# Attention: in the first step of each unit, TensorE takes the value products of the step before ahead of the turns

## The chip, the core and the metric

The kernel runs on one core of a Trainium2 chip. Time is device time in microseconds (us) from start to end of one execution. Five engines run their own instruction streams and meet only at semaphores: PE (TensorE, matrix products), DVE (VectorE), ACT (ScalarE), POOL (GpSimd) and SP (SyncE, here a DMA queue). "PEld" in the profile is PE's weight load, which overlaps its products.

## What is computed

One inference step of a hybrid decoder layer. The part that matters here is the attention over the prompt (1024 tokens, 8 query heads of 64, 2 KV heads), with three branches (compressed, selected, sliding window) whose softmax results are weighted by gates and added:

```
s = einsum('btkgd,bskd->bkgts', qg, win_kv[:, :, 0]) - slopes * d_w
p = masked_softmax(s, mask_w)
o_win = einsum('bkgts,bskd->btkgd', p, win_kv[:, :, 1])
...
o = g[:, :, 0] * o_cmp + g[:, :, 1] * o_slc + g[:, :, 2] * o_win
```

The other two branches have the same form over other keys. Around the attention lie the input projection, the convolution group, the compression of the cache, the output projection, an MLP and an embedding gate. Eight sampled sequences (32 rows) have their own attention, which is woven into the steps of the prompt's.

## The kernel before

The attention is the function `attend`. Its work on the prompt is cut into 32 **units** `(g, i)`: for each head pair `g` of 4, for each block `i` of 8 (128 query rows). Block `i` sees more keys the later it is, so a unit has 3, 5, 7, 9, 11, 12, 13 or 14 key blocks of 128. Two key blocks make a **group** `k`, two groups make a **step**; a unit has 1, 2, 2, 3, 3, 3, 4 or 4 steps (i = 0 to 7), 88 steps in all. Units are numbered 0 to 31, so unit 9 is `(1, 1)`; unit 8, 16 and 24 have one step only.

What each engine does for a group, in the order of the data:

- PE `qk(n+2, ch)` (L1815): scores of the unit after next, into one of two pairs of score banks; `score_banks` waits until DVE has read what stood there.
- DVE `scores` (L2076): adds the distance penalty, finds the row minimum, writes `S`.
- ACT `exps` (L1963): exponentials and their sums. ACT issues those of a step's scores one step later (the list `late`).
- DVE `weigh(n+1)` (L2086): reciprocals `inv` of the sums, in step 1 of unit `n` (step 0 if it has one step).
- POOL (L1782): scales `S` by `inv` and the gate, six instructions for a unit.
- PE `turn(k)` (L1827): transposes the scaled weights of a group, into one of three turn banks taken in rotation. It waits for POOL's scaling and for the bank of three turns ago to be kept.
- ACT (L1972, even `k`) or DVE (L2090, odd `k`) `keep(k)`: copies the turned bank to `PT`.
- PE `pv(k)` (L1839): value products, one instruction for each key block and KV head. The profile shows each as 2 records, so a full step of 4 key blocks is x16, and a single key block x4. It waits for `PT` to be kept; the first group of a unit also waits for `o_kept`, as all units sum into the same bank.
- ACT `keep_o(n)` (L1986): copies the finished bank to `mixA`. ACT issues it in the first step of unit `n+1`, behind that step's `keep`, the exponentials of the sampled rows and the late `exps`.

The sampled rows add to some steps: `turn_keys` (L1866, "tk"), kept by ACT (L1975) and DVE (L2093); `quad_scores` (L1874, "qs"), which takes a pair of score banks; `turn_weights` (L1883, "tw"), kept by ACT (L1978); `quad_values` (L1902, "qv"), which waits for that copy.

The order is written out by hand. Every engine takes its instructions in this order of steps; on PE a step `st` of unit `n` reads, cut:

```python
for k in steps[st]:
    turn(k)
...                       # turn_keys(z, 1), turn_weights(z)
for ch in share:
    qk(n + 2, ch)
for k in (steps[st - 1] if st else ()):
    pv(k)
...                       # turn_keys(z, 0), quad_scores, quad_values
```

So the value products of a step run one step late, behind the turns and the scores of the next one, and this holds across the border of two units too.

Of the kernel before, what the change touches and what calls it, by code (L numbers as in the profile page):

```python
# [1566 lines left out]
def attend(c, ps):  # L1567
# [60 lines left out]
    steps = [[m for m in range(a, min(a + 2, first_group[n + 1]))] for n in range(NU) for a in range(first_group[n], first_group[n + 1], 2)]  # L1628
# [4 lines left out]
    def with_step(n):  # L1633

        ns = first_step[n + 1] - first_step[n]
        nch = len(CHUNKS[n + 2]) if n + 2 < NU else 0
        return [[ch for ch in range(nch) if ch * ns // nch == j] for j in range(ns)]
# [7 lines left out]
    def quad_at(st, after_start):  # L1645

        return next((z for z in range(NZ) if START[z] + after_start == st), None)

    def weighed_at(st):

        return next((z for z in range(NZ) if START[z] + (4 if place(z) == 0 else 3) == st), None)

    def chosen_at(st, after_start):
        return next((gr for gr in range(2) if CHOOSE[gr] + after_start == st), None)
# [133 lines left out]
    def on_pe(pe):  # L1788
# [8 lines left out]
        def is_kept(t):  # L1797
            pe.wait_ge(kept[keeper(t)], keeps[turn_no[t]])
# [7 lines left out]
        def qk(n, ch):  # L1806
            g, i = UNITS[n]
            s = score_banks(("p", n, ch))
            off = 0
            for br, k0, w in CHUNKS[n][ch]:  # L1810
                for e in range(KVH):
                    rows = slice(DH * e, DH * e + DH)
                    w0 = P * max(0, i - 4)
                    keys = c.KcP[rows, :] if br == 0 else c.proj[rows, KS, k0:k0 + w] if br == 1 else c.proj[rows, KW, w0 + k0:w0 + k0 + w]
                    mm = nc.tensor.matmul(ps_S[:, s + e, off:off + w], c.q[rows, g, P * i:P * i + P], keys, start=True, stop=True)  # L1815
                off += w
            mm.then_inc(qk_done, 1)

        def turn(k):
            n, b0 = groups[k]  # L1820
            blocks = BLOCKS[n][b0:b0 + 2]
            if n:
                pe.wait_ge(scaled, 6 * n - 6 + max({1: 2, 2: 4, 0: 6}[br] for br, _, _ in blocks))
            ps = bank(("p", k))
            for j, (_, _, col) in enumerate(blocks):
                for e in range(KVH):
                    mm = nc.tensor.transpose(ps[:, P * (2 * j + e):P * (2 * j + e) + P], S[UNITS[n][1]][:, e, col:col + P], c.ident[:])  # L1827
            mm.then_inc(t_done, 1)

        def pv(k):  # L1830
            n, b0 = groups[k]
            is_kept(("p", k))
            if b0 == 0 and n:
                pe.wait_ge(o_kept, n)
            for j, (br, kb, _) in enumerate(BLOCKS[n][b0:b0 + 2]):
                for e in range(KVH):
                    rows = slice(DH * e, DH * e + DH)
                    v = c.VcP[:, rows] if br == 0 else c.V[:, kb, br - 1, rows]
                    mm = nc.tensor.matmul(ps_O[rows, 0:P], v, PTs[k % 4][:, P * (2 * j + e):P * (2 * j + e) + P],  # L1839
                                          start=(b0 + j == 0), stop=(b0 + j == len(BLOCKS[n]) - 1))  # L1840
            if k + 1 == first_group[n + 1]:
                mm.then_inc(pv_done, 1)

        def first_scores(gr):

            s = score_banks(("f", gr))
            for bb in range(GRP):
                b = GRP * gr + bb
                rows = slice(ROWS * bb, ROWS * bb + ROWS)
                nc.tensor.matmul(ps_S[rows, s, 0:256], c.QB[:, b, :], c.KcS[:, b, :], start=True, stop=True)  # L1850
                nc.tensor.matmul(ps_S[rows, s, 256:256 + SR], c.QB[:, b, :], c.KnT[:, 0, :], start=True, stop=True)
                mm = nc.tensor.matmul(ps_S[rows, s, 256 + SR:256 + 2 * SR], c.QB[:, b, :], c.KnT[:, 1, :], start=True, stop=True)
            mm.then_inc(qk_done, 1)

        def importance(gr):
            pe.wait_ge(imp_ready, gr + 1)
            ps = bank(("i", gr))
            nc.tensor.matmul(ps[:, 0:64], Gm[:], imp[:], start=True, stop=True).then_inc(t_done, 1)

        def turn_keys(z, half):  # L1860
            h = 2 * z + half
            pe.wait_ge(raw_loaded[h % 5], arrived(h))
            for bb in (2 * half, 2 * half + 1):
                ps = bank(("k", z, bb))
                for j in range(4):
                    mm = nc.tensor.transpose(ps[:, P * j:P * j + P], page(h, bb, j)[:, 0:P], c.ident[:])  # L1866
                mm.then_inc(t_done, 1)

        def quad_scores(z):
            s = score_banks(("s", z))  # L1870
            for bb in range(GRP):
                is_kept(("k", z, bb))
            for bb in range(GRP):
                mm = nc.tensor.matmul(ps_S[ROWS * bb:ROWS * bb + ROWS, s, :], c.QB[:, GRP * group_of(z) + bb, :], KT_[bb][:], start=True, stop=True)  # L1874
            mm.then_inc(qk_done, 1)

        def turn_weights(z):
            pe.wait_ge(sx_done, sx_after(z))
            if place(z) == 0:
                pe.wait_ge(win_scaled, group_of(z) + 1)  # L1880
            ps = bank(("q", z))
            for j in range(4):
                mm = nc.tensor.transpose(ps[:, P * j:P * j + P], Ss[z % 2][:, P * j:P * j + P], c.ident[:])  # L1883
            mm.then_inc(t_done, 1)
            if place(z) < 2:
                ps = bank(("n", z))
                for j, src in enumerate((Snew[:, 1, :], Pc[:, 0:P], Pc[:, P:2 * P]) if place(z) == 0 else (Snew[:, 0, :],)):
                    mm = nc.tensor.transpose(ps[:, P * j:P * j + P], src, c.ident[:])
                mm.then_inc(t_done, 1)

        def quad_values(z):
            gr = group_of(z)
            ps = bank(("o", z))
            is_kept(("q", z))
            more = []
            if place(z) < 2:
                is_kept(("n", z))
                more = [lambda b: c.Vn[:, 1, :], lambda b: c.VcS[:, 0, b, :], lambda b: c.VcS[:, 1, b, :]] if place(z) == 0 else [lambda b: c.Vn[:, 0, :]]
            for j in range(4):
                for bb in range(GRP):  # L1900
                    rows = slice(ROWS * bb, ROWS * bb + ROWS)
                    mm = nc.tensor.matmul(ps[rows, 0:P], PTq[:, j, rows], page(2 * z + bb // 2, bb, j)[:, P:2 * P],  # L1902
                                          start=(j == 0), stop=(j == 3 and not more))
            for j, v in enumerate(more):
                for bb in range(GRP):
                    rows = slice(ROWS * bb, ROWS * bb + ROWS)
                    mm = nc.tensor.matmul(ps[rows, 0:P], PTn[:, j, rows], v(GRP * gr + bb), start=False, stop=(j == len(more) - 1))
            mm.then_inc(t_done, 1)
# [6 lines left out]
        for n in range(NU):  # L1915
            for j, share in enumerate(with_step(n)):
                st = first_step[n] + j
                for k in steps[st]:
                    turn(k)
                z = quad_at(st, 1)  # L1920
                if z is not None:
                    turn_keys(z, 1)
                z = weighed_at(st)
                if z is not None:
                    turn_weights(z)
                for ch in share:
                    qk(n + 2, ch)
                for k in (steps[st - 1] if st else ()):
                    pv(k)
                z = quad_at(st, 0)  # L1930
                if z is not None:
                    turn_keys(z, 0)
                z = quad_at(st, 1)
                if z is not None:
                    quad_scores(z)
                gr = chosen_at(st, 0)
                if gr is not None:
                    first_scores(gr)
                z = weighed_at(st)
                if z is not None:  # L1940
                    quad_values(z)
                gr = chosen_at(st, 3)
                if gr is not None:
                    importance(gr)
                gr = joined_at(st, 5)
                if gr is not None:
                    turn_out(gr)
# [1762 lines left out]
```

## Time and profile before

| | us |
|---|---|
| median of 3 runs | 1820.42 |
| lowest and highest | 1818.45, 1823.94 |
| the profiled execution, its time | 1820.11 |
| its span, first to last instruction | 1818.5 |
| its granted TensorE clock, mean | 0.991 |
| PE busy in the span | 1760.1 (97%) |
| DVE, ACT, POOL busy | 1206.4, 767.0, 794.3 |
| the attention (`attend`), from and to | 549 to 890 |

The views used are the windows (busy time by engine in a stretch), the waits (who waited for whom, longest first in total) and the timeline (instructions in order of time; in brackets the idle time of the engine before the instruction, and what ended it). An idle time in the timeline is that of the engine; the end of a product is modelled, so the time PE loses is read best from start to start.

### The profile page before, as it was taken

The page shows a single profiled execution, that of the slowest core. Times are in us where ns is not written, and L with a number is a line of the kernel's source. Part 1 is how long each engine was busy: PE and PEld are TensorE (multiplying, and loading weights), DVE is VectorE, ACT ScalarE, POOL GpSimd, SP SyncE. Part 2 cuts the span into 40 slices and gives each one's busy share as a digit, 9 for nine tenths or more (in the row PEclk, how much of TensorE's full clock was granted, in tenths as well). Part 3 has the DMA queues.
Part 4 walks back from the last instruction along what each step waited for, and adds up shares of the span by engine and source line. Part 5 has one row for each costly group of instructions (what it writes and reads, how often), then busy time and mean ns, then how long its engine had stood idle before and what let it go on. Part 6 is the DMA issues. An engine that isn't in the chain of part 4 may idle for free.

```text
span 1818.5 us, 36980 instructions
## 1 busy us (share of the span) xinstructions
PE 1760.1 (97%) x14084; PEld 1639.8 (90%) x14084; DVE 1206.4 (66%) x1909; ACT 767.0 (42%) x1433; POOL 794.3 (44%) x763
## 2 busy tenths in 40 slices
PE   8999999999998999999999899999999999999998
PEld 7999998999995767676899899999999999999998
DVE  6799975675467676767746754555577878845535
ACT  5312332345345665666524333333433333314425
POOL 2204972224303433444544656556555444425531
PEclk9999999999999999999999999999999999999999
DMA  4321365536413444443314223222394632332214
GB/s 157 131 70 47 114 193 145 126 102 164 108 49 117 139 130 123 123 122 112 131 36 148 83 95 120 105 107 95 136 300 144 187 131 87 137 97 74 59 35 142
DMA packets 189983, 214.60 MB, mean 118 GB/s; under 512 B 23012, under 2 KB 152736, under 8 KB 189287
## 3 DMA queue, kind: packets, MB, share of 16 engines
q1 hardware_dynamic: 179357, 188.89, 33.3%
q0 software_dynamic: 7840, 21.25, 4.2%
q8 instruction: 112, 1.84, 0.4%
q10 hardware_dynamic: 2610, 2.10, 0.4%
q14 instruction: 64, 0.52, 0.1%
HBM read 181.22 MB, written 35.55 MB: 119 GB/s over the span
## 4 chain that ended last, share of the span: by engine, by line
PE 54%; DVE 7%; issue 3%; POOL 2%; ACT 2%; DMA 1%; SPq 0%; ACTq 0%; DVEq 0%; POOLq 0%
PE ps L2660 11%; PE ps L3039 8%; PE ps L2665 5%; PE ps L2420 4%; PE ps L3044 4%; PE ps L1827 3%; PE ps L3541 3%; PE ps L200 3%; PE ps L1839 3%; PE ps L1815 3%; POOL S L1782 2%; PE ps L1866 2%; PE ps L3551 1%; PE ps L206 1%; DVE S L2076 1%
## 5 line engine op out<-in xcount | busy, mean ns | idle before, releaser
L1782 POOL TENSOR_SCALAR S<-S,inv,gate_p 128x640 f32<-128x640 f32 (+7 forms) x186 | 124.9, 688 | 192.9 <-DVE inv L2086 192.9
L1166 DVE SCALAR_TENSOR_TENSOR y<-u,conv_w,y 128x1024 f32<-128x1024 f32 x120 | 156.5, 1351 | 1.2
L3039 PE MATMUL ps<-dn_op_hi,dn_hi 128*128 128x264 f32 x672 | 137.9, 287 | 6.8 <-DVE xT L3105 4.7
L433 POOL DMA_DIRECT2D raw<-in_cache_cmp_kv_dram x124 | 77.8, 630 | 151.1 <-DVE relaid L1252 122.4
L1010 PE MATMUL ps_p<-Xhi,w1hi 128*128 128x256 f32 x544 | 139.6, 294 | 1.4 <-ACT Xhi L715 1.4
L3039 PE MATMUL ps<-dn_op_lo,dn_hi 128*128 128x264 f32 x672 | 136.4, 284 | 0.0
L1010 PE MATMUL ps_p<-Xlo,w1hi 128*128 128x256 f32 x544 | 133.2, 284 | 0.0
L1236 DVE TENSOR_TENSOR Xlo<-ps_p,Xhi 128x512 fp32r<-128x512 f32 x132 | 85.1, 685 | 59.6 <-ACT Xhi L715 59.4
L715 ACT ACTIVATE Xhi<-ps_p 128x512 fp32r<-128x512 f32 x132 | 72.4, 598 | 105.5 <-PE ps_p L935 98.1
L3039 PEld LDWEIGHTS ps<-dn_op_hi,dn_hi 128*128 128x128 f32 x672 | 104.2, 189 | 9.2 <-DVE xT L3105 6.0
L1963 ACT ACTIVATE S<-S,mn 128x64 f32<-128x64 f32 (+8 forms) x180 | 108.7, 608 | 2.1 <-DVE mn L2076 2.1
L2660 PE MATMUL ps<-s_hi,up_hi 128*128 128x264 f32 x512 | 104.5, 286 | 3.0 <-ACT rstd L2630 3.0
L1010 PEld LDWEIGHTS ps_p<-Xhi,w1hi 128*128 128x128 f32 x544 | 103.8, 191 | 2.1 <-ACT Xhi L715 1.7
L864 PE MATMUL ps_p<-Ahi,win_hi 128*128 128x352 f32 x456 | 103.8, 327 | 1.5 <-DVE Alo L1143 1.5
L3039 PEld LDWEIGHTS ps<-dn_op_lo,dn_hi 128*128 128x128 f32 x672 | 104.5, 189 | 0.0
L2660 PE MATMUL ps<-s_lo,up_hi 128*128 128x264 f32 x512 | 104.2, 285 | 0.0
L1010 PEld LDWEIGHTS ps_p<-Xlo,w1hi 128*128 128x128 f32 x544 | 103.7, 191 | 0.0
L864 PE MATMUL ps_p<-Alo,win_hi 128*128 128x352 f32 x456 | 103.4, 326 | 0.0
L2974 POOL TENSOR_TENSOR dn_lo<-dn_t_sum,dn_hi 128x512 fp32r<-128x512 f32 x48 | 73.8, 1537 | 66.7 <-ACT dn_hi L2996 66.7
L1827 PEld LDWEIGHTS ps<-ident,S 128*128 128x128 f32 x592 | 64.0, 141 | 37.1 <-issue 19.9
L3044 PE MATMUL ps<-dn_op_hi,dn_lo 128*128 128x264 f32 x672 | 95.9, 285 | 0.0
L1827 PE MATMUL ps<-ident,S 128*128 128x128 f32 x592 | 85.4, 281 | 10.7 <-POOL S L1782 8.0
(502 smaller groups left out, 4911.7 us busy)
## 6 DMA issues: line engine op xcount, KB each, us to landing
s_raw<-in_cache_slc_kv_dram SPq DMA_DIRECT2D x256, 128.0 KB, 2.1
dn_op_raw<-hidden SPq DMA_DIRECT2D x21, 1056.0 KB, 6.3
raw<-in_cache_cmp_kv_dram SPq DMA_DIRECT2D x132, 128.0 KB, 4.2
hidden<-cs SPq DMA_DIRECT2D x32, 528.0 KB, 2.6
up_raw<-in_w_up_dram SPq DMA_DIRECT2D x16, 1024.0 KB, 5.5
raw<-in_cache_cmp_kv_dram POOLq DMA_DIRECT2D x124, 128.0 KB, 4.4
dn_w<-in_w_down_dram SPq DMA_DIRECT2D x48, 256.0 KB, 5.3
win_raw<-in_w_in_dram SPq DMA_DIRECT2D x38, 256.0 KB, 3.3
```

The costliest lines, as they stand in the source:

```text
L433: eng.dma_start(raw[s][DH * half:DH * half + DH, i, :], page.rearrange("o q f -> (o q) f")).then_inc(raw_loaded[0 if g < 2 else part][s], 16)
L864: mm = nc.tensor.matmul(ps[t % 2][:, j, 0:CH], w[t % 2][:, k, :], x[:, k, CH * j:CH * j + CH], start=(m == 0), stop=(m == NG - 1))
L1010: mm = nc.tensor.matmul(ps_h[n % 2][:, 0:w], ws[cc][:, j, :], x[n % 2][:, j % 8, slice(j // 8, j // 8 + w)], start=(j == 0 and m == 0), st ...
L1166: i = V_.scalar_tensor_tensor(out=y, in0=x, scalar=w, in1=y, op0=ALU.mult, op1=ALU.add)
L1236: V_.tensor_tensor(Xlo[n % 2][x], ps_x[v % 2].rearrange("p (n j) -> p j n", j=8), Xhi[n % 2][x].bitcast(F32), ALU.subtract).then_inc(lo_re ...
L1782: nc.gpsimd.tensor_scalar(x, x, inv[:, n % 3, 3 * e + br:3 * e + br + 1], c.gate_p[:, i, H * br + h:H * br + h + 1], ALU.mult, ALU.mult).t ...
L1827: mm = nc.tensor.transpose(ps[:, P * (2 * j + e):P * (2 * j + e) + P], S[UNITS[n][1]][:, e, col:col + P], c.ident[:])
L1963: nc.scalar.activation(x, x, ACT.Exp, bias=mn[:, n % 3, e, br, part:part + 1], scale=-1.0, accum_out=sums[:, n % 3, 3 * e + br:3 * e + br ...
L2660: nc.tensor.matmul(ps[:, bank + j, 0:HC], w_hi[s % 4][:, k, :], ops[m][:, k, c0 + HC * j:c0 + HC * j + HC], start=(k == 0 and m == 0), sto ...
L2665: mm = nc.tensor.matmul(ps[:, bank + j, 0:HC], w_lo[s % 4][:, k, :], ops[0][:, k, c0 + HC * j:c0 + HC * j + HC], start=False, stop=(k == K ...
L3039: nc.tensor.matmul(ps[:, 2 * m + j, 0:HC], w_hi[q % 4][:, k, :], x[:, k, HC * j:HC * j + HC], start=(k == 0 and x is op_hi[n]), stop=False)
L3044: mm = nc.tensor.matmul(ps[:, 2 * m + j, 0:HC], w_lo[q % 4][:, k, :], op_hi[n][:, k, HC * j:HC * j + HC], start=False, stop=(k == KH - 1))
```

## The change

In the first step of each unit but the very first, the loop that issues `pv` for the step before stands ahead of the turns. In all other steps it stays behind the scores. Nothing is added or removed: the same instructions with the same waits, in another order on PE. ACT, DVE, POOL and SP keep theirs.

```diff
             for j, share in enumerate(with_step(n)):
                 st = first_step[n] + j
+                opens = j == 0 and st > 0
+                if opens:
+                    for k in steps[st - 1]:
+                        pv(k)
                 for k in steps[st]:
                     turn(k)
...
                 for ch in share:
                     qk(n + 2, ch)
-                for k in (steps[st - 1] if st else ()):
+                for k in (steps[st - 1] if st and not opens else ()):
                     pv(k)
```

## Rows read from the trace of the kernel before

**Rows 1.** Windows: length, busy us of PE, PEld, DVE, ACT, POOL; clock; DMA.

```profile
549.00:890.00 341.00, 321.81 (x3472) 227.45 (x3473) 243.42 (x806) 221.63 (x601) 147.82 (x217) 0.99 0.40 121
584.00:637.00 53.00, 52.09 (x627) 38.67 (x622) 35.78 (x113) 33.64 (x94) 21.91 (x31) 1.00 0.40 121
```

**Rows 2.** Waits from 545 to 890: who for whom, us in total, times, longest.

```profile
PE ps L1827 <- POOL S L1782: 8.0, 11, 1.3
PE ps L1839 <- ACT mixA L1986: 3.5, 5, 1.5
ACT mixA L1986 <- PE ps L1839: 14.0, 16, 2.2
```

**Rows 3.** Timeline of PE and ACT, first and second step of unit 9: start, us, instruction.

```profile
643.34 1.09 PE L1827 MATMUL ps<-ident,S 128*128 128x128 f32 x8
644.03 0.60 ACT L1972 ACTIVATE PT<-ps 128x512 f32<-128x512 f32 x1 [1.75 <-PE ps L1827]
644.37 1.99 PE L1815 MATMUL ps<-proj,q_back 64*128 64x512 f32 x8
...
646.28 0.66 PE L1839 MATMUL ps<-PT,V 128*64 128x128 f32 x8
...
647.09 0.44 PE L1827 MATMUL ps<-ident,S 128*128 128x128 f32 x2
...
648.67 0.25 ACT L1986 ACTIVATE mixA<-ps 128x128 f32<-128x128 f32 x1
...
649.07 1.09 PE L1839 MATMUL ps<-PT,V 128*64 128x128 f32 x16 [0.73 <-ACT mixA L1986]
```

**Rows 4.** Timeline of PE and ACT, first and second step of unit 6.

```profile
613.12 1.09 PE L1827 MATMUL ps<-ident,S 128*128 128x128 f32 x8
613.82 0.60 ACT L1972 ACTIVATE PT<-ps 128x512 f32<-128x512 f32 x1 [3.04 <-PE ps L1827]
617.68 0.26 ACT L1986 ACTIVATE mixA<-ps 128x128 f32<-128x128 f32 x1
618.08 1.09 PE L1839 MATMUL ps<-PT,V 128*64 128x128 f32 x16 [0.56 <-ACT mixA L1986]
```

**Rows 5.** Timeline, first step of unit 4: its turns, and the copy before them.

```profile
584.49 1.09 PE L1827 MATMUL ps<-ident,S 128*128 128x128 f32 x8
585.25 0.41 DVE L2090 COPY PT<-ps 128x256 f32<-128x256 f32 x1
```

**Rows 6.** Timeline, first step of unit 12: scores, their reading, value products, quad scores.

```profile
674.43 1.77 PE L1815 MATMUL ps<-proj,q_back 64*128 64x512 f32 x8
675.61 0.75 DVE L2076 CUSTOM_DVE_ANT_0 S<-ps,far_selected,neg_slope 128x512 f32<-128x512 f32 x1 [0.38 <-PE ps L1815]
676.30 0.44 PE L1839 MATMUL ps<-PT,VcP 128*64 128x128 f32 x4
677.09 1.07 PE L1874 MATMUL ps<-s_KT,QB 128*32 128x512 f32 x8 [0.35 <-DVE mn L2076]
```

**Rows 7.** Timeline, unit 21: DVE's scores, its key copy, the key turns after it.

```profile
777.26 0.75 DVE L2076 CUSTOM_DVE_ANT_0 S<-ps,far_selected,neg_slope 128x512 f32<-128x512 f32 x1 [0.31 <-PE ps L1815]
780.08 0.69 DVE L2093 COPY s_KT<-ps 128x512 f32<-128x512 f32 x1
780.91 1.07 PE L1866 MATMUL ps<-ident,s_raw 128*128 128x128 f32 x8
```

**Rows 8.** Timeline, end of unit 18 and the turns that open unit 19.

```profile
748.13 1.09 PE L1839 MATMUL ps<-PT,V 128*64 128x128 f32 x16
750.51 1.09 PE L1827 MATMUL ps<-ident,S 128*128 128x128 f32 x8 [1.30 <-POOL S L1782]
```

**Rows 9.** Timeline, first step of unit 30: weights turned, kept, used.

```profile
872.59 0.60 PE L1883 MATMUL ps<-ident,s_S 128*128 128x128 f32 x4
873.22 0.60 ACT L1978 ACTIVATE s_PTq<-ps 128x512 f32<-128x512 f32 x1 [0.28 <-PE ps L1883]
874.14 1.08 PE L1902 MATMUL ps<-s_raw,s_PTq 128*32 128x128 f32 x32
```

## Prediction

> **What bounds the kernel now.** I read the windows first, then PE's waits, then the timeline around each of the 31 unit borders. The windows show the attention as a stretch of 341.00 us in which PE is busy for 321.81 us, while DVE, ACT and POOL have 243.42, 221.63 and 147.82 us of work [rows 1]. So the attention is set by PE's in-order stream and the 19.2 us in which it stands still. The waits name two of these that the change touches: turns that wait for POOL's scaling, 8.0 us in 11 places, and the first value products of a unit that wait for ACT's copy of the unit before, 3.5 us in 5 places [rows 2]. Outside the attention no instruction changes place.
>
> **What is moved, and its length.** Turns of a full step hold PE from 643.34 to 644.37, 1.03 us; two full score chunks 1.91 us; value products of three key blocks 0.81 us (646.28 to 647.09) [rows 3]. A full step of products shows 1.09 us, whose last 0.06 to 0.07 overlaps what follows, so 1.02 us. By key blocks the move carries at each border: 0.54 (i=0), 0.81 (i=1), 0.37 (i=2), 0.81 (i=3), 0.37 (i=4), 0.81 (i=5), 1.02 (i=6), 0.37 (i=7). The short ones are estimates by key block. Summed over 31 borders this is 19.7 us of PE work ahead of turns and scores. PE's total work is the same; what changes is that turns and scores come later by the moved length, and that nothing stands any more between the scores and what follows them. Each has a price where another engine had no slack.
>
> **Gain: waits that are filled.** At unit 19 the last products start at 748.13 and are issued by 749.15; the turns start at 750.51, held by POOL [rows 8]. The 0.81 us of products fit in these 1.36 us. Going border by border, such a wait exists at units 2, 3, 10, 17, 19, 25, 26 and 27, and min(wait, moved length) sums to 4.6 us. That is the whole intended gain, since POOL's wait is only 8.0 us in all [rows 2], and part of it lies at turns that open no unit.
>
> **Cost 1: the result copy comes later.** In unit 9's first step ACT idles 1.75 us for the turn, then works without a gap until the copy of unit 8's result at 648.67, and PE's first products of unit 9 start right behind it at 649.07, after 0.73 us of waiting [rows 3]. That copy shows no wait for the products it copies: ACT is what is late, through `keep` and the late exponentials, all behind the turn. With 0.81 us of products ahead of the turn, ACT's chain and those products come 0.81 later. In unit 6 it is the same with 1.02 us: idle 3.04 before 613.82, copy at 617.68, products at 618.08 [rows 4]. Only 16 of 31 copies wait for PE [rows 2]; at these the move helps ACT by as much, and nothing is lost. Of the other 15 most have slack. Priced with each one's slack: unit 1 0.81, unit 6 1.02, unit 9 0.81, unit 11 0.13, unit 14 1.01, unit 22 0.62 (it returns as a wait for a turn bank two steps on).
> The Trainium skill's page "PSUM — Partial Sum Buffer" says under "Engine vs sequencer instructions" that ScalarE's queue is strictly first in, first out. By that rule the copy can't pass the exponentials, and the price stands; if it could, this term of about 4.4 us would be nothing and the sum about 3.3 us over the time before. The rows agree with the rule.
>
> **Cost 2: the preceding step isn't kept yet.** At 584.49 PE is ready to open unit 4. The last group of unit 3 is kept by DVE from 585.25 to 585.66 [rows 5]. Before, that was needed only behind two score chunks; now PE waits 1.3 us with everything behind it. Some 0.3 of this comes back at the next turns, so 1.0 us. At all other borders the copies end 0.3 us or more before PE arrives.
>
> **Cost 3: score banks.** In unit 12's first step the quad scores at 677.09 already wait for DVE to read the first chunk, which DVE begins 1.18 us behind the start of the scores at 674.43 [rows 6]. The 0.37 us of products at 676.30 covered part of this wait. Moved ahead, they push the scores and the reading 0.37 later and cover nothing: plus 0.37, likewise at units 18 and 20; at unit 8 0.54. At unit 26 the filled 0.37 is lost to the same wait.
>
> **Cost 4: turn banks behind DVE.** In unit 21 DVE goes from the scores at 777.26 without a gap to the key copy at 780.08; the next key turns start at 780.91, as that bank is free [rows 7]. Scores 0.81 later give 0.78, likewise in unit 29. In unit 10 the stretch is of this kind too (0.1 net).
>
> **Cost 5: the tail.** In unit 30 there are no scores. The turned weights (872.59) are copied by ACT from 873.22 to 873.82, and PE uses them at 874.14, behind the value products that now lie ahead [rows 9]. The copy comes 1.02 later and ends at 874.84, so PE waits until 874.96: 0.82. POOL's last scaling, which sets the end of the attention, moves with it. Unit 31 has slack and costs nothing.
>
> **Sum, cycle by cycle** (a filled wait counts only if nothing behind it gives it back):
> - units 1 to 7: 0.81 lost at unit 1, given back by filled waits at 2 and 3; plus 1.00 (unit 4) plus 1.02 (unit 6): 2.0
> - units 8 to 15: 0.54 + 0.81 + 0.10 + 0.13 + 0.37 + 1.01: 3.0
> - units 16 to 23: the fill at 17 is swallowed by DVE's load in the next step, 0.37 at 18, minus 0.81 at 19, then 0.37 + 0.78 + 0.62: 1.3
> - units 24 to 31: about 0.6 by unit 26 (later copies and scores), minus 0.81 at 27, then 0.78 + 0.82: 1.4
>
> Together 7.7 us slower. Against the profiled execution's 1820.11, which is 0.31 below the median, this gives 1827.8; against the median 1828.1. I take 1828.0, 0.42% up. Behind the attention comes the output projection, where PE is busy without a gap, so nothing there takes it back.
>
> **The rivals.**
> *A, the border is filled and nothing is behind it.* If ACT and DVE have more slack than their gapless stretches suggest, the 4.6 us stand, and the earlier end of a unit's products also frees the result copy, which would remove the 3.5 us of [rows 2]: 1820.4 - 8.1 = 1812.3. It decides where ACT's copies waited for PE; 16 did, but the five that hold PE did not [rows 3, 4]. Chance 0.06.
> *B, absorbed.* Half or more of the shifts vanish in waits that end on their own, or fills hold where I let them be swallowed: between 1815 and 1825.8, at the middle 1821. Of PE's 19.2 us of idle time 11 are outside the two waits named, which speaks for it; that ACT and DVE are themselves started by PE there speaks against it. Chance 0.32.
> *C, every shift is paid in full.* 19.7 us less 4.6 gives 1835. Against it stand the 16 copies that wait for PE. Chance 0.06.
> *D, the clock.* Around the borders turns now follow turns more closely. The granted clock is 1.00 in a stretch that holds seven borders [rows 1]. The Trainium skill's page "TensorE: Matmul & The Clock Gate" says under "Part 4: PE-mode transpose" that transposes don't count as activity for the clock. By it long runs of turns would drop PE to 1.2 GHz. Without the page: a border of about 5 us at half the clock costs up to 5 us, and at a few of them the time would be about 1845. Such runs of turns and key turns stand in that stretch already at full clock. Chance 0.01.
>
> **Chances and range.** Forecast (1825.9 to 1832) 0.55, A 0.06, B 0.32, C 0.06, D 0.01. A measurement of this kernel can tell some 0.3% (5.5 us) from no change: slower 0.62, same 0.32, faster 0.06. The range reaches into B and C: 1818.5 to 1834.
>
> **What would show it.** Right: the first products of units 6, 9 and 14 start 0.8 to 1.0 later behind their turns, PE's wait for the result copy (3.5 us) grows to 7 or more, its wait for POOL (8.0) shrinks to about 4; the products that open unit 4 wait 1.3 us for DVE; quad scores in units 8, 12, 18 and 20 wait longer for DVE. Wrong: copies that start no later than before, or an attention no longer than 341 us. The prediction falls above all if ACT's exponentials start on something other than the turn.

## The result, and the profile after

The changed kernel takes 1827.65 us (median of 6, 1824.1 to 1829.74) against 1820.02 (6 runs of the kernel before, beside them): ratio 1.0032, 95% interval 1.0019 to 1.0046, slower by 3.5 to 8.4 us. The two medians lie 7.6 us apart; the middle of the interval is 5.8 us. Predicted were 1828.0. Its profiled execution has 1826.1 us and a span of 1824.4.

The windows of the attention after the change (columns as in [rows 1]: length, busy time of PE, PEld, DVE, ACT, POOL with counts, clock, DMA):

```profile
549.00:896.50 347.50, 319.68 (x3460) 227.40 (x3462) 242.63 (x806) 218.24 (x600) 147.19 (x217) 1.00 0.40 117
```

The window grew from 341.0 to 347.5 us. Both are cut at round times; from the attention's first turn to the first product of the output projection it is 340.59 before and 347.54 after. PE's work did not grow (321.81 in [rows 1], part of it at a lower clock, 319.68 here); its idle time did, from 19.2 to 27.8. PE's waits from 545 to 900 (who for whom, us in total, times, longest; those that changed most) say where:

```profile
PE ps L1839 <- ACT mixA L1990: 7.8, 8, 1.9
PE ps L1874 <- DVE mn L2080: 3.8, 5, 1.0
PE ps L1827 <- POOL S L1782: 3.2, 6, 0.6
PE ps L1866 <- DVE s_KT L2097: 3.2, 3, 1.5
PE ps L1902 <- ACT s_PTq L1982: 2.1, 3, 0.8
PE ps L1839 <- DVE PT L2094: 1.2, 1, 1.2
PE ps L1827 <- DVE PT L2094: 1.0, 1, 1.0
PE ps L1827 <- DVE mixA L2172: 0.6, 1, 0.6
```

Lines behind the diff are 4 higher than before: L1990 is the copy of the result that was L1986. Against [rows 2], the turns' wait for POOL fell from 8.0 to 3.2 us. Not all of these 4.8 us are gain. At the openings of units 3, 17, 19, 26 and 27 it shrank by 3.5, which the moved products filled. At unit 2 another 1.05 went because PE came there late and at a lower clock (last section), at unit 31 0.87 because PE now waits for DVE there, and at unit 22 0.61 is new. The wait for the result copy rose from 3.5 to 7.8, and quad scores (L1874) waiting for DVE rose from 1.8 (before) to 3.8, in 5 places both times. Key turns waiting for DVE (L1866 behind `s_KT`) rose from 1.1 to 3.2, and a wait of 1.2 for DVE's `PT` in front of value products is new, as are the last two lines, the turns of unit 31 behind DVE. What was filled is paid back more than twice over. The first products of unit 4, the quad scores of unit 12 and the key turns of unit 21 show one each of these waits:

```profile
585.54 0.44 PE L1839 MATMUL ps<-PT,VcP 128*64 128x128 f32 x4 [1.23 <-DVE PT L2094]
680.79 1.06 PE L1874 MATMUL ps<-s_KT,QB 128*32 128x512 f32 x8 [0.72 <-DVE mn L2080]
786.89 1.07 PE L1866 MATMUL ps<-ident,s_raw 128*128 128x128 f32 x8 [0.84 <-DVE s_KT L2097]
```

Unit 6 shows one price in full. PE and ACT, first and second step (start, us, instruction; in brackets the idle time before it and what ended it):

```profile
614.67 1.09 PE L1827 MATMUL ps<-ident,S 128*128 128x128 f32 x8
615.37 0.60 ACT L1976 ACTIVATE PT<-ps 128x512 f32<-128x512 f32 x1 [4.06 <-PE ps L1827]
619.22 0.26 ACT L1990 ACTIVATE mixA<-ps 128x128 f32<-128x128 f32 x1
619.62 1.09 PE L1839 MATMUL ps<-PT,V 128*64 128x128 f32 x16 [1.58 <-ACT mixA L1990]
```

Against [rows 4]: ACT starts 0.70 us behind the turn in both, and the copy starts 3.85 (before 3.86) behind that. Only PE changed places: it has nothing left to do behind the scores and waits 1.58 instead of 0.56. The difference, 1.02, is the length of the moved products. So the unit's first products do not start later behind its turns (4.95 us, before 4.96): turns, copy and products are all 1.02 late together.

**The lag table.** The timeline gives the start of the turns of each of the 88 steps. The lag of a step is its start in a kernel less its start in before, less the same difference at the attention's first turn. What a border costs is the change of the lag across its unit, counted from the end of unit 0 on. Two profiled executions of one order agree in this to about 0.02 us per unit, with a drift of 0.15 over the whole attention, apart from a few places where the granted clock falls (e0_none, below). By groups of units:

| units | forecast | measured |
|---|---|---|
| 1 to 7 | +2.0 | +2.40 |
| 8 to 15 | +3.0 | +3.16 |
| 16 to 23 | +1.3 | +1.28 |
| 24 to 31 | +1.4 | +1.46 |
| sum | +7.7 | +8.30 |

The first product of the output projection comes at 897.19 instead of 889.59. These 7.60 us are the 8.30, plus 0.65 by which the attention's first turn was late (549.65 instead of 549.00), less 1.35 that before's profile loses in unit 0, where its granted clock is 0.54.

### The profile page after: what moved, and what is told of

Same layout as the page of the kernel before. It is cut to its first block, busy times and chain, and to the rows that moved or that the text cites. A ratio compares the mean times of both kernels' runs of the same rounds, so it can differ in the third digit from the quotient of the medians.

```text
span 1824.4 us, 36980 instructions
## 1 busy us (share of the span) xinstructions
PE 1759.5 (96%) x14084; PEld 1640.6 (90%) x14084; DVE 1206.7 (66%) x1909; ACT 764.8 (42%) x1433; POOL 794.4 (44%) x763
## 4 chain that ended last, share of the span: by engine, by line
PE 54%; DVE 8%; issue 4%; POOL 2%; ACT 2%; ACTq 0%; DVEq 0%; POOLq 0%
PE ps L2664 11%; PE ps L3043 8%; PE ps L2669 6%; PE ps L2424 4%; PE ps L3048 4%; PE ps L3545 3%; PE ps L200 3%; PE ps L1839 3%; PE ps L1827 3%; PE ps L1815 2%; POOL S L1782 2%; PE ps L3555 1%; PE ps L206 1%; DVE S L2080 1%; PE ps L1866 1%
```

## The experiments

The theories: the **ledger** of the prediction (each border has its own price, by what another engine lacks there), the **spread** theory (the loss is a share of all the work moved, 0.39, wherever it is moved), and the **absorbed** theory. The absorbed theory is the prediction's rival B: most shifts vanish in waits that end on their own.

The kernel before ran again beside each experiment: 35 runs with a median of 1820.43 us for e1_copy to e4_copy_first, 27 with 1819.14 for e0_none, e5_split and e6_rest, 9 with 1820.3 for the other two. The ratios are taken against these and need not be the quotient of the two medians.

First, partial kernels, each with the early opening at some borders alone. The edit is one line, with the list of units changed:

```diff
-                opens = j == 0 and st > 0
+                opens = j == 0 and n in (1, 6, 9, 14, 22)
```

**e1_copy**: the borders at which the result copy is late.

> Only units 1, 6, 9, 14 and 22 open with the preceding step's value products; the other 26 borders are as before. These are the borders where the ledger says that ACT's copy of the preceding unit's result comes later by the whole moved length. Ledger theory: the start of the turns two steps behind the border lags the kernel before by 0.81 (unit 1), 1.02 (unit 6), 0.81 (unit 9), 1.01 (unit 14) and 0.4 to 0.6 us (unit 22) more than ahead of it, about 4.1 to 4.3 us in all, so 1820.0 + 4.2 = 1824.2, with nothing lost anywhere else. Spread theory: the loss of 7.6 us is not tied to places but is a share of all the work moved (7.6 of 19.7 us, 0.39); with 4.4 us moved here it gives 1.7 us, so 1821.7. Absorbed theory: 1820.0 or less.

Measured: 1822.04 us (12 runs), ratio 1.0009, interval 0.9997 to 1.0022: as a time it can't be told from nothing. The lags can: unit 1 +0.98, unit 6 +1.01, unit 9 +0.78, unit 14 +1.01, unit 22 +0.36, in all 4.08 us, and 0.00 to 0.03 in every unit between. The ledger holds (4.1 to 4.3), the spread theory (1.7) falls. Unit 22 is at 0.36, not 0.62.

**e2_banks**: list (4, 8, 12, 18, 20, 21, 29, 30).

> Only units 4, 8, 12, 18, 20, 21, 29 and 30 open early: the borders that the ledger prices for DVE's keeping of the preceding step (unit 4, 1.00), for score banks (unit 8 0.54; 12, 18 and 20 0.37 each), for turn banks (21 and 29, 0.78 each) and for the tail (30, 0.82). Ledger theory: these lags, 5.0 us in all, so 1825.0. Spread theory: 4.8 us moved times 0.39 is 1.9 us, so 1821.9. If the costs of the ledger existed only because the borders ahead of them had shifted the engines against each other, units 8, 12, 18, 20, 21 would show less than half of their lags here.

Measured: 1825.09 us (12 runs), ratio 1.0026, interval 1.0013 to 1.0038. Lags: unit 4 +0.85, 8 +0.58, 12 +0.37, 18 +0.38, 20 +0.35, 21 +0.81, 29 +0.66, unit 30 to the end +1.43; in all 5.41. The borders pay the same when the ones ahead of them are undone, so these are prices of places. Unit 30 has 0.6 more than the ledger. Where that comes from can be seen on DVE, whose subtractions for the output projection (`y_lo`) stand among its copies of turned groups. The first two of them in the timeline of before, then in that of e2_banks:

```profile
877.27 1.26 DVE L2215 TENSOR_TENSOR y_lo<-y,y_hi 128x1056 fp32r<-128x1056 f32 x1 [0.15 <-ACT y_hi L2032]
879.17 1.45 DVE L2215 TENSOR_TENSOR y_lo<-y,y_hi 128x1056 fp32r<-128x1056 f32 x1
```

```profile
879.47 2.07 DVE L2219 TENSOR_TENSOR y_lo<-y,y_hi 128x1056 fp32r<-128x1056 f32 x1 [0.34 <-ACT y_hi L2036]
882.06 1.65 DVE L2219 TENSOR_TENSOR y_lo<-y,y_hi 128x1056 fp32r<-128x1056 f32 x1
```

The same two instructions take 1.0 us longer in sum, and the turns of unit 31 wait for a bank behind them:

```profile
884.65 0.63 PE L1827 MATMUL ps<-ident,S 128*128 128x128 f32 x4 [0.81 <-DVE mixA L2172]
886.68 0.63 PE L1827 MATMUL ps<-ident,S 128*128 128x128 f32 x4 [0.45 <-DVE PT L2094]
```

The changed kernel has 2.06 and 1.65 too; all the kernels that leave unit 30 alone have 1.26 and 1.45. In e4_copy_first (below), where unit 30 opens early but ACT is ordered otherwise, they take 1.29 and 1.43, and the 0.6 is not there: unit 30 to the end costs 0.65.

What differs is POOL's first scaling (for unit 31), which begins just ahead of the first subtraction. In before, then in e2_banks:

```profile
877.21 2.30 POOL L1782 TENSOR_SCALAR S<-S,inv,gate_p 128x1024 f32<-128x1024 f32 x1 [5.64 <-DVE inv L2086]
```

```profile
879.24 1.20 POOL L1782 TENSOR_SCALAR S<-S,inv,gate_p 128x1024 f32<-128x1024 f32 x1 [6.33 <-DVE inv L2090]
```

When it begins 0.06 us ahead (before) or 0.08 (e4_copy_first, 2.27 us long), POOL's instruction is the long one and DVE's takes 1.26 to 1.29. When it begins 0.23 or 0.24 ahead, as in e2_banks and the changed kernel, POOL's takes 1.20 and DVE's is the long one. It looks as if one of the two stands still while the other runs, and 0.2 us of timing decide which; the spans of POOL are rough, and no run was made to test this.

**e3_fill**: list (3, 19, 27).

> Only units 3, 19 and 27 open early: the borders at which a wait of PE for POOL's scaling is filled by the moved products and nothing behind gives it back. Ledger theory: minus 0.81 us at each, minus 2.4 in all, so 1817.6. Spread theory: plus 0.9 us (0.39 of 2.4 moved), so 1820.9. The two differ in sign, and the lags in the trace (to about 0.01 us) tell them apart even where the times do not.

Measured: 1816.41 us (12 runs), ratio 0.9981, interval 0.9969 to 0.9994. Lags: -0.80, -0.81, -0.81; behind unit 3, 0.31 comes back at unit 4; in all -2.22. The sign decides against the spread theory. The turns that open unit 19, which waited 1.30 in [rows 8], here start behind the products:

```profile
745.28 1.53 PE L1839 MATMUL ps<-PT,V 128*64 128x128 f32 x24
746.65 0.39 PE L1839 MATMUL ps<-PT,VcP 128*64 128x128 f32 x4
747.67 1.09 PE L1827 MATMUL ps<-ident,S 128*128 128x128 f32 x8 [0.64 <-POOL S L1782]
```

**e6_rest**: the fifteen other borders.

> The fifteen borders that the three partial kernels left out open early: units 2, 5, 7, 10, 11, 13, 15, 16, 17, 23, 24, 25, 26, 28, 31. Ledger: unit 2 minus 0.4, units 10 and 11 plus 0.2 together, 24 to 26 plus 0.6, all others 0 (fills there are given back a step or two later, other shifts fall into slack): plus 0.5 us in all. From the changed kernel's own lags, if they are additive: 10 and 11 plus 0.3, 16 and 17 plus 0.4, 24 to 26 plus 0.2, units 7 and 15 plus 0.15, units 5 and 23 minus 0.15 to 0.2: plus 0.8. Spread theory: 8.1 us moved times 0.39 is 3.2 us, so 1823.2. If the parts are additive, the lags of the four partial kernels add up to that of the changed kernel within 0.5 us.

Measured: 1818.46 us (10 runs, spread from 1817 to 1826), ratio 1.0009, interval 0.9995 to 1.0023: no change that the times can tell. Lags: unit 2 -0.01, 5 -0.15, 7 +0.15, 10 and 11 together +0.26, 13 0.00, 15 +0.15, 16 and 17 together +0.37, 23 -0.20, 24 to 26 together +0.19, 28 and 31 0.0; in all +0.67. The four partial kernels give 4.08 + 5.41 - 2.22 + 0.67 = 7.94 of the whole change's 8.30: the prices add up to within 0.4 us. Of the rest, 0.13 is there by unit 4, where borders of different partial kernels stand side by side; the other 0.2 gathers slowly over the remaining units, which is no more than the drift between profiles.

**e0_none**: list (), so the order of before, to see how far two executions of it differ.

> No border opens early: the order of every engine's work is that of the kernel before. This measures what two profiled executions of one order differ by. Step by step through the attention, the lags against the profile of before should be within 0.02 us, except at the start of the attention, where before's profile shows a granted clock of 0.54 for 3 us that three other kernels' profiles with the same order there do not show: if that is chance, this profile is 1.35 us ahead from the first unit on; if it belongs to the order of before, it shows it too. Median 1820.0 within the interval.

Measured: 1821.36 us (10 runs), ratio 1.0011, interval 0.9998 to 1.0024. So an order that is the same can stand 0.1% apart here. My expectation missed: the profile is not 1.35 us ahead but 0.63 behind in unit 0, and loses another 1.50 in unit 3, where nothing was changed. From unit 4 to the end the lags move by 0.13 in all. Windows of 3 us (the clock is the third number from the end):

```profile
549.00:552.00 3.00, 3.00 (x15) 2.07 (x15) 0.45 (x2) 0.60 (x1) 2.94 (x10) 0.50 0.77 214
552.00:555.00 3.00, 2.71 (x15) 0.91 (x15) 2.62 (x12) 0.00 (x0) 0.24 (x1) 0.57 1.09 357
576.00:579.00 3.00, 3.00 (x14) 1.44 (x14) 0.78 (x2) 2.26 (x6) 0.40 (x2) 0.59 0.00 0
```

Both losses are stretches of some 3 to 6 us at the lower clock, which come and go between executions.

**e8_single**: list (1, 17, 26).

> Units 1, 17 and 26 alone open early. Unit 1: all three profiles in which it opened early had a granted clock near 0.5 for about 3 us right behind its wait of 1.5 to 1.95 us, the others had none at that place; if the early opening brings it, it is there again and unit 1 costs 1.0; if it was chance, unit 1 costs 0.8 at most and the clock stays 1.00. Unit 17 and unit 26: the ledger says 0 for each (at 17 the fill of POOL's wait is given back behind DVE in the next step, at 26 it is lost to the score bank); if they are real fills, minus 0.8 and minus 0.37. The lags of the group 16 and 17 (plus 0.37) and 24 to 26 (plus 0.19) would then belong to units 16, 24 and 25.

Measured: one time, 1817.9 us, which says little; the lags say it. Unit 1: -1.36 to -0.35, so +1.0, with the lower clock there again. Unit 17: +0.08. Unit 26: 0.00. The ledger's two swallowed fills are right. By subtraction, 0.3 of the +0.37 of 16 and 17 belongs to unit 16, and the +0.19 of 24 to 26 to units 24 and 25, none of which was opened alone. PE at unit 1, and its window:

```profile
560.30 1.97 PE L1839 MATMUL ps<-PT,V 128*64 128x128 f32 x16 [1.95 <-ACT mixA L1990]
562.21 1.76 PE L1827 MATMUL ps<-ident,S 128*128 128x128 f32 x8
```

```profile
561.00:564.00 3.00, 3.00 (x22) 2.33 (x19) 2.12 (x5) 2.83 (x9) 3.00 (x6) 0.57 0.48 144
```

**e4_copy_first**: the changed kernel, with ACT's copy ahead of its other work in a unit's first step.

```diff
                 st = first_step[n] + j
+                copy_first = j == 0 and n
+                if copy_first:
+                    keep_o(n - 1)
                 for k in steps[st]:
                     if k % 2 == 0:
                         keep(k)
...
-                if j == 0 and n:
+                if j == 0 and n and not copy_first:
                     keep_o(n - 1)
```

> All borders open early, as in the changed kernel, and besides ACT's copy of the preceding unit's result is put at the very front of ACT's work of the unit's first step, ahead of ACT's keeping of the turned groups. Everything else is the changed kernel. If the five waits for the copy (7.8 us in 8 places in the changed kernel) arise because the copy stands behind ACT's late work and not because it waits for the products, they shrink to a small rest, since the products it copies are now complete at the border's very front. Ledger theory: minus 1 to 1.7 us at units 6 and 14 each against the changed kernel, minus 0.4 to 0.6 at unit 22, between 0 and minus 0.3 at units 1 and 9, where what the copy delays (ACT's keeping, its exponentials, then POOL's scaling) is needed soon; about 4 us below the changed kernel, 1823.6. If the copy's own length (0.4 to 0.5 us) is in the way wherever it stands, no gain: 1827.6. If the copy waits for PE at the front and holds ACT's keeping behind it, slower than the changed kernel.

Measured: 1825.74 us (12 runs), ratio 1.0030, interval 1.0020 to 1.0041. Of the 4 us expected the lags show 0.9 (7.39 instead of 8.30), and little of it comes from the copy. From unit 4 on it is 1.7, of which 0.77 are the tail (DVE's short subtractions, above) and 0.2 each unit 6 and unit 22; unit 14 gains nothing. Units 1 to 3 lose 0.8 against the changed kernel: there the clock fell under the scores for unit 4, which took 3.23 us instead of 1.78. The wait for the copy is gone from the list, yet PE waits nearly as long. Unit 6:

```profile
613.75 0.28 ACT L1990 ACTIVATE mixA<-ps 128x128 f32<-128x128 f32 x1 [3.49 <-PE ps L1839]
618.18 0.58 ACT L1976 ACTIVATE PT<-ps 128x512 f32<-128x512 f32 x1
618.65 0.59 ACT L1982 ACTIVATE s_PTq<-ps 128x512 f32<-128x512 f32 x1
616.93 1.09 PE L1839 MATMUL ps<-PT,V 128*64 128x128 f32 x16
619.38 1.08 PE L1902 MATMUL ps<-s_raw,s_PTq 128*32 128x128 f32 x32 [1.36 <-ACT s_PTq L1982]
```

The copy is early (613.75) and the products no longer wait (616.93). But the copy was only the first of three things behind ACT's late exponentials. The keeping of the next turned group and of the turned weights stand there too, and PE needs them 1 us later: the wait of 1.58 for the copy became one of 1.36 for `s_PTq`. In unit 9 it is 1.10, in unit 14 1.36. The step that was wrong: I took the copy's wait as the price and did not ask what stands behind the copy on ACT.

**e5_split**: the test that follows from this. Units 3, 6, 19 and 27 open early. In the first step of units 6 and 14, ACT's last two exponentials are held back, and come behind the copy and the two keepings. An added argument `part` of `exps` makes it do all but the last two (0), or the last two (1):

```diff
+                if j == 1 and n in (6, 14):
+                    exps(*held_job, 1)
                 z = quad_at(st, 2)
                 if z is not None:
                     quad_exps(z)
+                held = late[-1:] if j == 0 and n in (6, 14) else []
                 for m, ch in late:
-                    exps(m, ch)
+                    exps(m, ch, 0 if (m, ch) in held else None)
```

> Units 3, 19 and 27 open early (minus 0.81 each, as measured with these alone), and unit 6 too. In the first step of units 6 and 14 the last two exponentials (the two of 64 columns, 0.33 us each) are taken out of ACT's late work and come one step later, behind the copy of the preceding unit's result, the keeping and the turned weights. Unit 14 does not open early. If ACT's late exponentials are what makes the copy late, every wait for it shrinks by the 0.66 us taken out: unit 6 opens with a wait of 0.9 instead of 1.58 and lags before by 0.36 instead of 1.02, with no new wait for the turned weights behind it; unit 14, not opened early, loses its wait of 0.57 and gains 0.5 on before. Attention minus 2.4 plus 0.36 minus 0.5 is minus 2.6 us: about 1817.5. If the copy waits for something else (the products, the bank), unit 6 stays at 1.02 and unit 14 at 0: minus 1.4.

Measured: 1816.08 us (11 runs), ratio 0.9990, interval 0.9979 to 1.0001. Lags: unit 6 +0.36, as expected to 0.01; unit 14 -0.76 (expected -0.5; the wait of 0.56 for POOL in that unit's last step is gone as well); all together -2.84 from unit 1 on. In unit 6 (its start of the copy, and the products' wait):

```profile
614.35 0.26 ACT L1992 ACTIVATE mixA<-ps 128x128 f32<-128x128 f32 x1
614.75 1.09 PE L1839 MATMUL ps<-PT,V 128*64 128x128 f32 x16 [0.92 <-ACT mixA L1992]
615.77 1.08 PE L1902 MATMUL ps<-s_raw,s_PTq 128*32 128x128 f32 x32
```

Taking 0.66 us of exponentials away from ahead of the copy took 0.66 us off its wait (1.58 to 0.92), and no wait for the weights came in its place. This shows the prediction's Cost 1 directly: ACT's queue is what is late, not the products. The Trainium skill's page "PSUM — Partial Sum Buffer" ("Engine vs sequencer instructions") says that ScalarE's queue is strictly first in, first out. The traces agree: e4_copy_first and e5_split moved the copy only by moving it, or what stands ahead of it, in the program.

**e7_best**: only what gained. Units 3, 5, 19, 23 and 27 open early; units 6 and 14 do not, and have the held-back exponentials.

> Only what gained so far, together: units 3, 5, 19, 23 and 27 open early (measured lags, from the partial kernels and, for 23, the changed kernel: minus 0.8, 0.15, 0.8, 0.2, 0.8; some of unit 3's may come back at unit 4), and in the first steps of units 6 and 14, which do not open early, the last two exponentials go behind the copy (minus 0.56 to 0.66 at unit 6, where before waits 0.56 for the copy, and minus 0.76 as measured at unit 14). If the parts add: 3.7 to 4.1 us less than before from the first unit on. On the clock's good or bad start of the attention another 0 to 2 us depend in a single profile. Time 1816, ratio 0.9978. If the parts don't add, less than 2.5.

Measured: 1815.87 us (5 runs) against 1820.3 (9 runs of before), ratio 0.9965, interval 0.9951 to 0.9978: a little faster than the kernel before, and so than the changed one. Lags from unit 1 on: -0.80 (unit 3), +0.08 (4), -0.15, -0.63 (6), -0.76 (14), -0.82, -0.20, -0.81, in all -4.17. PE's waits:

```profile
PE ps L1827 <- POOL S L1782: 5.3, 10, 1.0
PE ps L1839 <- ACT mixA L1992: 2.4, 3, 1.5
```

POOL's 8.0 fell to 5.3 and the copy's 3.5 to 2.4. Quad scores wait 1.8 and key turns 1.1 for DVE, as before; one wait of 0.4 of a turn for DVE is new.

## Why the prediction was right, point by point

**Where it stood.** The forecast, 1828.0, is 0.35 us off. That is luck in part: the interval of the ratio spans 5 us, and errors of the ledger cancel. What carries is the table of groups above, where no group is off by more than 0.4 us, and below it the borders one by one; inside the last group plus 0.6 and minus 0.4 cancel too. In the first group 0.45 is a fall of the clock (last section) that no term foresaw; without it the group would be at +1.95.

**Gain.** Filled waits of 4.6 us were forecast, and POOL's wait shrank by 4.8, but that these two agree is chance: only 3.5 of the 4.8 stand at openings that fill a wait. Units 3, 19 and 27 keep theirs (-0.81 each, e3_fill). The fills at units 17 and 26 are swallowed, as the ledger had it (e8_single: +0.08 and 0.00). Missed: units 5 and 23 gain 0.15 and 0.20, where I had nothing.

**Cost 1, the copy.** Units 6, 9 and 14 cost 1.01, 0.78 and 1.01 against 1.02, 0.81 and 1.01. Mis-sized terms: unit 22, 0.36 instead of 0.62, and unit 1, 1.0 instead of 0.81 (the 0.2 is the clock). The mechanism is shown by e5_split. One sign was put wrongly: the first products of units 6, 9 and 14 were to start 0.8 to 1.0 later behind their turns. They start as before (4.95, 5.72 and 4.95 us behind them), since the turns come late by the same length. What the prediction said of the mechanism was too narrow, though: not only the copy is behind the exponentials, and e4_copy_first is the price of thinking so.

**Cost 2, unit 4.** PE waits 1.2 for DVE's keeping of the last group of unit 3 (1.3 forecast); after what comes back, 0.85 to 0.92 instead of 1.00.

**Cost 3, score banks.** Units 12, 18 and 20: 0.37, 0.38, 0.35 against 0.37 each. Unit 8: 0.58 against 0.54. Missed: unit 16, with the same small unit behind it as unit 8 (i = 7 to i = 0), some 0.3 (by subtraction), where I had taken the shift as absorbed.

**Cost 4, turn banks.** Unit 21 0.81 against 0.78, unit 29 0.66 against 0.78. Units 10 and 11 0.26 against 0.23.

**Cost 5, the tail.** The wait for the turned weights in unit 30 is 0.78, as forecast to 0.04. What failed is the step after it: I followed the delay to POOL's last scaling and not to DVE. DVE's first two subtractions take 1.0 us longer in this order, and the turns of unit 31 wait 0.59 and 0.96 for DVE behind them, and no longer for POOL. Opening unit 31 alone costs nothing (e6_rest), as forecast. Unit 30 to the end costs 1.41 to 1.43 instead of 0.82. Opposite to it, the 0.6 for units 24 to 26 is 0.2.

**The rivals.** A is out: the copies that held PE did not come earlier, they held it longer. B had its point: of 19.7 us moved, e6_rest's 8.1 cost only 0.67. But the ledger had counted that slack already. One argument for B was misread: outside the two waits named lie 19.2 - 8.0 - 3.5 = 7.7 us of idle time, not 11. C is out by the same numbers. (The lengths per border in the prediction add up to 19.9 us, not 19.7; nothing hangs on it.) D, the clock, had a chance of 0.01 and happened at one border of 31, though not by the mechanism that I gave it. Its argument was weaker than it says: the stretch of [rows 1] from 584 to 637 holds four borders, not seven. Runs of turns kept the clock: it is 1.00 in the changed kernel from 584 to 897, also from 783.99 to 787.96, where PE does nothing but turns and waits 0.84 between them. The Trainium skill's page "TensorE: Matmul & The Clock Gate" ("Part 4: PE-mode transpose") has transposes not count as activity in the way products do. In these windows no run of turns brought a fall. But none is longer than 4.5 us, waits included, before products follow, so what a longer run would do no trace here shows. At unit 1 the clock fell behind a wait of PE.

## What to carry to other kernels

Moving work on the bound engine ahead in its own queue costs nothing in work and can still lose: each filled wait is worth min(wait, moved length), and each engine that hangs on what was pushed back, and works without a gap until its next result is needed, charges the moved length, less what slack it has (1.01 of 1.02 at unit 6, 0.36 of 1.02 at unit 22). Price each place by itself; in this kernel places interact little (within 0.4 of 8.3 us), so the winners can be kept and the losers dropped (e3_fill, e7_best). When a wait ends at an instruction in another engine's queue, look at what stands ahead of that instruction and at what stands behind it: moving the instruction alone only hands the wait to the next one (e4_copy_first); moving what is ahead of all of them removes it (e5_split).

## What the runs showed of the hardware

**The clock falls behind a wait at unit 1, each time that it opens early.** In all four profiles with that opening (the changed kernel, e1_copy, e4_copy_first, e8_single) a 3-us window from 561 or 564 has a granted clock of 0.51 to 0.68, for a while at the lower of the two levels (0.50, 1.2 GHz); in the seven without it, it is 1.00 there. In three of the four PE had just waited 1.94 or 1.95 us, in e4_copy_first 1.52, 0.45 and 0.77 with short work between. Four against seven is what the runs show; what brings the fall is not tested. The windows of e1_copy:

```profile
558.00:561.00 3.00, 0.76 (x8) 0.65 (x10) 2.15 (x11) 3.00 (x13) 0.30 (x1) 0.92 0.60 180
561.00:564.00 3.00, 3.00 (x23) 2.50 (x20) 1.92 (x6) 3.00 (x10) 3.00 (x6) 0.51 0.42 143
```

Sixteen product records took 1.97 us instead of 1.09, and eight turns 1.74 to 1.76 instead of 1.09, together 1.5 us more. In e1_copy and e8_single only 0.2 of it stayed in the lag (unit 1 costs 1.0 against a moved length of 0.81), as PE would have waited for POOL next. In before, from those products to the scores for unit 4:

```profile
562.02 1.09 PE L1839 MATMUL ps<-PT,V 128*64 128x128 f32 x16 [1.52 <-ACT mixA L1986]
563.41 0.66 PE L1827 MATMUL ps<-ident,S 128*128 128x128 f32 x4 [0.29 <-POOL S L1782]
564.82 0.66 PE L1827 MATMUL ps<-ident,S 128*128 128x128 f32 x4 [0.76 <-POOL S L1782]
565.41 1.78 PE L1815 MATMUL ps<-proj,q_back 64*128 64x512 f32 x12
```

In the changed kernel, where unit 2 opens early too:

```profile
562.12 1.98 PE L1839 MATMUL ps<-PT,V 128*64 128x128 f32 x16 [1.95 <-ACT mixA L1990]
563.86 0.67 PE L1839 MATMUL ps<-PT,VcP 128*64 128x128 f32 x4
564.46 1.57 PE L1827 MATMUL ps<-ident,S 128*128 128x128 f32 x8
565.96 1.78 PE L1815 MATMUL ps<-proj,q_back 64*128 64x512 f32 x12
```

The way from the products to the scores is 3.84 us instead of 3.39. At full clock the 0.35 us of unit 1's last products would have fitted into POOL's waits, so the fall costs 0.45 here; that is worked out, not measured. Waits of 1.5 us at units 6, 9 and 14 of the changed kernel, with PE busy around them, brought no fall.

**Some falls come and go with the same order.** At the attention's start, 549 to 555, three of eleven profiles have windows with a clock of 0.50 to 0.57 (before 0.54, e0_none, e7_best) and the others 1.00, though all have the same order of work there or nearly so; it costs 1.4 to 2.0 us. The profile of before, on which the prediction rests, is one of the three: it is 1.35 us slower there than the eight others. The fall at 576 in e0_none stands in no other profile. That is part of why a change of 0.2% is read from lags within one stage, and not from two times.
